# Seven-product couples in the down projection: two or four per FFN group, block products kept in PSUM over a layer

## What is computed

```python
def hybrid_layer(x, ...):
    ...
    x = x + rms_norm(mixed, g_mix_post)
    f = jnp.square(jax.nn.relu(rms_norm(x, g_ffn_pre) @ w_up)) @ w_down
    return x + rms_norm(f, g_ffn_post)

def reference(x, ...):
    for l in range(DEPTH):
        x = hybrid_layer(x, ...)
    return x
```

## Time and profile before

| | |
|---|---|
| median of 3 runs | 1924.66 us (1924.56 to 1925.11) |
| the profiled execution | 1924.85 us, span of its instructions 1923.0 us |
| busy | PE 1904.1 us (99%), VectorE 1376.1 (72%), ScalarE 951.4 (49%), GpSimd 139.6 (7%) |
| mean granted TensorE clock | 0.999 |
| HBM read | 377.55 MB, 197 GB/s over the span |

### The profile page before, as it was taken

How to read it: one execution, slowest core, us unless ns; L and a number is a source line. 1 busy time by engine, 2 the same in 40 slices (tenths; PEclk the granted TensorE clock), 3 DMA queues, 4 the chain that set the end, 5 groups by cost and what they waited for, 6 DMA issues and landing times.

```text
span 1923.0 us, 28285 instructions
## 1 busy us (share of the span) xinstructions
PE 1904.1 (99%) x10070; PEld 1695.4 (88%) x10070; DVE 1376.1 (72%) x1637; ACT 951.4 (49%) x1249; POOL 139.6 (7%) x178
## 2 busy tenths in 40 slices
PE   9999999999999999999999999999999999999998
PEld 7988888888988988898888888889889889989987
DVE  6885767875785686578778757678657757856785
ACT  6455656543453444345454556556434434444452
POOL 3920020000000000000200000200000000000002
PEclk9999999999999999999999999999999999999999
DMA  8665356666666566666476544566766765666664
GB/s 286 207 225 171 125 171 219 198 226 189 190 225 206 177 207 219 182 205 218 159 240 219 182 163 147 186 210 198 228 188 190 227 197 183 205 222 185 200 207 139
DMA packets 168324, 380.78 MB, mean 198 GB/s; under 512 B 11968, under 2 KB 14128, under 8 KB 167728
## 3 DMA queue, kind: packets, MB, share of 16 engines
q1 hardware_dynamic: 167904, 377.58, 61.2%
q10 hardware_dynamic: 336, 2.11, 0.3%
HBM read 377.55 MB, written 2.10 MB: 197 GB/s over the span
## 4 chain that ended last, share of the span: by engine, by line
PE 89%; DVE 6%; issue 2%; ACT 1%; DMA 1%; POOL 0%; DVEq 0%; ACTq 0%; POOLq 0%; SPq 0%
PE acc_pair L530 22%; PE acc_pair L535 11%; PE acc_pair L829 9%; PE acc_pair L831 9%; PE acc_pair L830 9%; PE acc_pair L496 8%; PE acc_pair L498 8%; PE acc_pair L497 8%; DVE w_lo L1319 2%; ACT w_hi L938 1%; DVE act_f L1785 1%; PE o_bank L748 1%; DVE h_both L1373 1%; DVE x L1354 0%; PE t_bank L729 0%
## 5 line engine op out<-in xcount | busy, mean ns | idle before, releaser
L1319 DVE TENSOR_TENSOR w_lo<-raw,w_hi 128x1024 fp32r<-128x1024 f32 x703 | 862.1, 1245 | 352.7 <-ACT w_hi L938 344.1
L938 ACT CAST w_hi<-raw 128x1024 fp32r<-128x1024 f32 x703 | 722.5, 1049 | 504.6 <-PE acc_pair L831 231.1
L530 PE MATMUL acc_pair<-h_both,w_hi 128*128 128x512 f32 x2176 | 561.1, 380 | 5.4 <-DVE act_f L1785 5.3
L530 PEld LDWEIGHTS acc_pair<-h_both,w_hi 128*128 128x128 f32 x2176 | 371.3, 191 | 37.0 <-DVE act_f L1785 6.9
L535 PEld LDWEIGHTS acc_pair<-h_both,w_lo 128*128 128x128 f32 x2176 | 327.6, 191 | 29.0
L535 PE MATMUL acc_pair<-h_both,w_lo 128*128 128x256 f32 x2176 | 330.6, 274 | 0.0
L829 PE MATMUL acc_pair<-w_hi,f_hi 128*128 128x512 f32 x784 | 297.3, 379 | 0.0
L830 PE MATMUL acc_pair<-w_lo,f_hi 128*128 128x512 f32 x784 | 297.3, 379 | 0.0
L831 PE MATMUL acc_pair<-w_hi,f_lo 128*128 128x512 f32 x784 | 297.2, 379 | 0.0
L496 PE MATMUL acc_pair<-w_hi,h_both 128*128 128x512 f32 x444 | 170.5, 384 | 1.4 <-DVE w_lo L1319 1.2
L498 PE MATMUL acc_pair<-w_hi,h_both 128*128 128x512 f32 x444 | 168.3, 379 | 0.0
(11 more groups left out here) (247 smaller groups left out, 1586.1 us busy)
## 6 DMA issues: line engine op xcount, KB each, us to landing
raw<-in_w_up SPq DMA_DIRECT2D x256, 512.0 KB, 4.3
raw<-in_w_down SPq DMA_DIRECT2D x256, 512.0 KB, 4.7
raw<-in_w_in SPq DMA_DIRECT2D x128, 512.0 KB, 4.8
raw<-in_w_out SPq DMA_DIRECT2D x64, 512.0 KB, 5.2
x<-in_x SPq DMA_DIRECT2D x8, 256.0 KB, 7.7
w_pool_s<-in_w_pool SPq DMA_DIRECT2D x2, 1024.0 KB, 7.9
post_row<-in_g_mix_post SPq DMA_DIRECT2D x2, 1024.0 KB, 7.8
post_row<-in_g_ffn_post ACTq DMA_DIRECT2D x2, 1024.0 KB, 8.1
```

Source lines behind the costliest of these rows:

```text
L530: pe.matmul(acc_pair[b][:, m, :], w_hi[:, slot, col:col + P], x_both.rearrange("p s (a n) -> p s n a", a=2), start=(slot, k) == (0, 0), st ...
L938: act.copy(w_hi[:, half * PAIRS + p, :], raw[:, p, :]).then_inc(hi_made, 1)
L1319: dve.tensor_tensor(w_lo[:, slot, :], raw[:, p, :], w_hi[:, slot, :].bitcast(F32), ALU.subtract).then_inc(lo_made, 1)
```

## The change

It puts four couples into the first wide pair, at blocks 0, 4, 8 and 12, with the row blocks reordered so that their f blocks are ready. s tiles get four copies, t tiles stay one set. The four shared products accumulate in their PSUM banks over the four groups of a layer (start in group 0, stop in the last couple of group 3). `p_sums` is gone. In the last group ScalarE copies two of the banks to `q_sum`, and `combine` reads the other two from PSUM; it now stands behind `wide_sums` and two lows. In `seven`, the products that need t tiles come after the four that don't. In up units VectorE does the second bank's reduction after one low in place of two and s_lo; in the last unit the second half's lows move behind all of it, into `seven_lo` of couple 1.

```diff
-SEVEN_AT = (0, RING)
-K_ORDER = ((4, 5, 0, 1, 2, 3, 8, 9, 6, 7, 10, 11, 12, 13, 14, 15), tuple(range(2 * RING)))
+SEVEN_AT = (0, PAIRS, RING, RING + PAIRS)
+SEVEN_UNIT = ((1, 0), (1, 1), (2, 0), (2, 1))
+K_ORDER = ((4, 5, 0, 1, 6, 7, 2, 3, 8, 9, 12, 13, 10, 11, 14, 15), tuple(range(2 * RING)))
...
@@ tensor: seven
-                    first, last = n == 0, n == len(SEVEN_AT) - 1
+                    first = n == 0
+                    p_first = first and isinstance(g, int) and g == 0
+                    p_last = isinstance(g, int) and g == FF_GROUPS - 1 and n == len(SEVEN_AT) - 1
...
-                    pe.wait_ge(t_lo_made, no + 1)
-                    if first and not (isinstance(g, int) and l + g == 0):
-                        pe.wait_ge(p_free, 4 * (l * FF_GROUPS + g))
-                    three(t_bank[1][:, :], sh[:, 0, :], sl[:, 0, :], t_hi[:, 0, :], t_lo[:, 0, :],
-                          first, last)
-                    three(o_bank[:, :], sh[:, 1, :], sl[:, 1, :], t_hi[:, 1, :], t_lo[:, 1, :],
-                          first, last)
...
+                    pe.wait_ge(t_lo_made, no + 1)
+                    three(t_bank[1][:, :], sh[:, 0, :], sl[:, 0, :], t_hi[:, 0, :], t_lo[:, 0, :],
+                          p_first, p_last)
+                    three(o_bank[:, :], sh[:, 1, :], sl[:, 1, :], t_hi[:, 1, :], t_lo[:, 1, :],
+                          p_first, p_last)
...
@@ scalar: turned_unit, group
+                    if (u, 0) in SEVEN_UNIT:
+                        split_hi(hu + 3, 1, (0, 1, 2))
+                        s_rest(g, SEVEN_UNIT.index((u, 0)))
+                        split_hi(hu + 3, 1, (3,))
+                    elif u < CHUNKS - 1:
                         split_hi(hu + 3, 1)
                     turned_hi(g, u, 1)
+                    if u == CHUNKS - 1:
+                        s_rest(g, 3)
+                        seven_hi(g, 1, hu + 3, 1)
...
-                    seven_hi(g, 1, hu + 10)
-                    for n in range(1, PAIR_HALVES if last else 2 * PAIR_HALVES):
+                    seven_hi(g, 2, hu + 10, 0)
+                    seven_hi(g, 3, hu + 11, 1)
+                    for n in range(2, PAIR_HALVES if last else 2 * PAIR_HALVES):
                         split_hi(hu + 8 + n + 2, n % 2)
                     if not last:
                         return
+                    act.wait_ge(t_used, seven_no(l, g, len(SEVEN_AT)))
+                    for k, bank in ((0, t_bank[0]), (1, t_bank[1])):
+                        act.copy(halves(q_sum[:, k, :]), put_back(bank[:, :])).then_inc(p_copied, 1)
...
@@ vector: combine, wide_pair, turned_unit
-                    dve.wait_ge(p_free, 4 * FF_GROUPS * (l + 1))
+                    dve.wait_ge(p_copied, 2 * (l + 1))
+                    for t in range(T):
+                        dve.wait_ge(acc_free[t], 1 + a0 + ACC_F + 8 * FF_GROUPS - 2)
...
-                        seven_lo(g, 1, hu + 2)
-                        split_lo(hu + 3, 1)
-                        split_lo(hu + 4, 0, (0, 1))
-                        p_sums(g, first)
-                        split_lo(hu + 4, 0, (2, 3))
-                        if last:
-                            combine()
+                        seven_lo(g, 2, hu + 2, 0)
+                        seven_lo(g, 3, hu + 3, 1)
+                        split_lo(hu + 4, 0)
...
                     wide_sums(g, j, first)
                     split_lo(hu + PAIR_HALVES + 1, 1, (2, 3))
+                    if last:
+                        combine()
...
-                        split_lo(hu + u * 2 + 3, 1, (1, 2))
-                        if u == 1:
-                            s_rest(g, 0)
+                        if u < CHUNKS - 1:
+                            split_lo(hu + u * 2 + 3, 1, (1,))
                         turned_square(g, u, 1)
-                        split_lo(hu + u * 2 + 3, 1, (3,))
+                        if u < CHUNKS - 1:
+                            split_lo(hu + u * 2 + 3, 1, (2,))
+                        if (u, 0) in SEVEN_UNIT:
+                            s_rest(g, SEVEN_UNIT.index((u, 0)))
+                        if u < CHUNKS - 1:
+                            split_lo(hu + u * 2 + 3, 1, (3,))
                         turned_lo(g, u, 1)
-                        if u == 1:
-                            s_sums(g, 1)
+                        if (u, 1) in SEVEN_UNIT:
+                            s_sums(g, SEVEN_UNIT.index((u, 1)))
+                        if u == CHUNKS - 1:
+                            s_rest(g, 3)
+                            seven_lo(g, 1, hu + u * 2 + 3, 1)
```

More of the change, by code:

```diff
@@ L231, in build @@
     t_lo = at("t_lo", [P, 3, CH], F32R, r_qkv + 24 * CH)
[L232 to L235, removed]
+    r_s = ((r_qkv + 36 * CH, r_qkv + 40 * CH), (r_qkv + 44 * CH, r_xg), (r_xg + 4 * CH, r_post),
+           (r_post + 4 * CH, r_post + 8 * CH))
+    s_hi = [at(f"s_hi{n}", [P, 4, P], F32R, hi) for n, (hi, _) in enumerate(r_s)]
+    s_sum = [at(f"s_sum{n}", [P, 4, P], F32, low) for n, (_, low) in enumerate(r_s)]
+    s_lo = [at(f"s_lo{n}", [P, 4, P], F32R, low) for n, (_, low) in enumerate(r_s)]
     ident = own("ident", [P, P])
@@ L844, in seven @@
                     pe.wait_ge(lo_made, (hu + i // PAIRS) * PAIRS + 2 + RAW)
-                    pe.wait_ge(t_lo_made, no + 1)
-                    if first and not (isinstance(g, int) and l + g == 0):
-                        pe.wait_ge(p_free, 4 * (l * FF_GROUPS + g))
-                    three(t_bank[1][:, :], sh[:, 0, :], sl[:, 0, :], t_hi[:, 0, :], t_lo[:, 0, :],
-                          first, last)
-                    three(o_bank[:, :], sh[:, 1, :], sl[:, 1, :], t_hi[:, 1, :], t_lo[:, 1, :],
-                          first, last)
                     three(ssa_bank[:, :], sh[:, 2, :], sl[:, 2, :], w_hi[:, s0, right],
-                          w_lo[:, s0, right], first, last)
+                          w_lo[:, s0, right], p_first, p_last)
                     three(t_bank[0][:, :], f_hi[:, k0, early], f_lo[:, k0, early], w_hi[:, s0, left],
-                          w_lo[:, s0, left], first, last).then_inc(w_used, 1)
+                          w_lo[:, s0, left], p_first, p_last).then_inc(w_used, 1)
                     if first:
@@ L1229, in s_rest, with seven_hi @@
                     act.copy(s_hi[n][:, :, :], s_sum[n][:, :, :]).then_inc(s_hi_made, 1)
[L1231 to L1235, removed]
+                def seven_hi(g, n, hu, half):
+                    no = seven_no(l, g, n)
+                    act.wait_ge(t_third, no + 1)
+                    split_hi(hu, half, (0, 1))
+                    act.wait_ge(t_step, 3 * no + 3)
                     act.copy(t_hi[:, :, :], t_sum[:, :, :]).then_inc(t_hi_made, 1)
-                    split_hi(hu, 0, (2, 3))
+                    split_hi(hu, half, (2, 3))
                 def turned_unit(g, u, hu):
                     if u == CHUNKS - 1:
-                        seven_hi(g, 0, hu + 2)
+                        seven_hi(g, 0, hu + 2, 0)
                     elif u == 2:
@@ L1853, in s_rest, with seven_lo @@
                                       ).then_inc(s_lo_made, 1)
-                def seven_lo(g, n, hu):
+                def seven_lo(g, n, hu, half):
                     no = seven_no(l, g, n)
@@ L1872, in seven_lo @@
                                       ).then_inc(t_step, 1)
-                    split_lo(hu, 0, (0, 1))
+                    split_lo(hu, half, (0, 1))
                     dve.wait_ge(t_hi_made, no + 1)
@@ L1876, in seven_lo @@
                                       ALU.subtract).then_inc(t_lo_made, 1)
[L1877 to L1888, removed]
+                    split_lo(hu, half, (2, 3))
                 def combine():
                     q1, q5, q6, q7 = (q_sum[:, k, :] for k in range(4))
-                    dve.wait_ge(p_free, 4 * FF_GROUPS * (l + 1))
+                    dve.wait_ge(p_copied, 2 * (l + 1))
+                    for t in range(T):
+                        dve.wait_ge(acc_free[t], 1 + a0 + ACC_F + 8 * FF_GROUPS - 2)
                     def into(t, c, part):
@@ L1898, in into @@
                                                  ALU.mult, ALU.add).then_inc(q_step, 1)
-                    dve.tensor_tensor(q6, q6, q1, ALU.add).then_inc(q_step, 1)
+                    dve.tensor_tensor(halves(q6), put_back(o_bank[:, :]), halves(q1), ALU.add
+                                      ).then_inc(q_step, 1)
                     into(0, 0, q1)
                     dve.wait_ge(q_step, 8 * l + 1)
-                    dve.tensor_tensor(q7, q7, q6, ALU.add).then_inc(q_step, 1)
+                    dve.tensor_tensor(halves(q7), put_back(ssa_bank[:, :]), halves(q6), ALU.add
+                                      ).then_inc(q_step, 1)
                     dve.tensor_tensor(q6, q6, q5, ALU.add).then_inc(q_step, 1)
```

20 lines of the change are left out of this document (8 added, 12 removed).

## The result

| | before | after |
|---|---|---|
| median | 1924.61 us (1924.09 to 1925.11) | 1977.56 us (1976.39 to 1978.26, 4 runs) |
| the profiled execution | 1924.85 us, span 1923.0 | 1976.39 us, span 1974.6 |
| mean granted TensorE clock | 0.999 | 0.985 |

The ratio is 1.0275 [1.0257, 1.0292]: 53 us slower, where 34 were forecast. The time lies in the range, near the 1981 us of rival 1.

A forecast was written before the change was run, and what follows sets the result against it. PE bounds the kernel, by its count of matmuls plus few gaps. Against 1924.85 us: -10.4 (matmuls) -5.3 (up units) +4.8 (couples) +45.0 (standstills) = +34.1, so 1959 us; range 1938 to 1985.

The forecast's parts named there:

- rival 1: PE's clock falls to half pace behind each wide-pair standstill, 2.7 us more each, 22 in all: 1981 us; chance 0.32.
- Matmuls: In the two more couples of each of 8 groups, 48 fewer matmuls take 10.4 us off PE.
- Up units: VectorE reduces unit 1's second bank earlier, closing eight PE gaps of 0.66 us: 5.3 us off.
- Couples: In the first wide pair, PE slips 0.2 us at each of three couples per group: 4.8 us on.
- Standstill: After the first wide pair, PE waits for sums behind six lows: 5.7 us, 5.4 more in last groups; 45.0 on.
- point (e): Expected sign in the trace: a group takes about 170.8 us, against 166.41 before.
- rival 2: Loads land sooner or the chain has slack, so wide-pair standstills shrink to VectorE's own work: 1928 us; chance 0.10.
- The clock: Behind wide-pair standstills, the forecast's own case kept PE at full clock and charged nothing for a fall.
- The last group: In each layer's last group, combine behind the sums stays hidden: 0, at worst 1 us per layer.
- Rival 3: VectorE keeps its lead, lows do not delay the sums; only matmuls and eight gaps count: 1909 us; chance 0.06.

The follow-up runs named there:

- The version of 1913.61 us: Changed kernel with first wide pair's sums after two lows, combine two lows after them, bank copies before most casts, first narrow sum behind one low: 1913.61 us.
- the last experiment: The version of 1913.61 us with block 1's cast and low of each couple moved ahead of VectorE's wait for t_used: 1944.68 us.

## Why the prediction was right in sign and 19 us short

- **Matmuls** (-10.4): right; 48 are gone, and the experiments' sums close with it to within some 2 us.
- **Up units** (5.3): the mechanism was right, the size was not; 7.8. I multiplied the idle time that the rows print. The time lost is start against due start, 0.93 us and not 0.66.
- **Couples** (0.2 us each, 4.8): 0.19 in the mean, 4.5 in all. In the group shown the heads come 10.12 and twice 9.95 us apart (550.08, 560.20, 570.15) against 9.71; the head waits for a low, and `t_lo` for the moved products is hidden, as worked out.
- **Standstill** (5.7 us, in the last groups 5.4): 5.84 by the row, 6.0 from ready to start (5.4 to 6.2 over the eight), at the place and by the chain foretold. VectorE met `t_used` 4.84 us behind the first head and 4.95 behind the second (565.15 against 560.20), where I had 4.8; low 6 ended at W + 45.1 where I had 44.3. From the end of one such gap to that of the next are 173.1 us (422.79, 595.92): the 170.8 of point (e), 1.9 of clock behind the first of them, and 0.4 more. The loads landed as the earlier trace rows had them, in 5.1 us in the median here against 5.0; no run shortened them, so their part in the 6 us rests on the timeline. The Trainium skill's page "DMA: Bandwidth & Descriptors" (Anatomy of one DMA) gives its 2.0 us plus bytes at 436 GB/s for DMAs that GpSimd's path issues, and these loads go by SyncE's hardware queue, which the prediction passed over. With that figure, by my estimate 3.2 us for 512 KB, rival 2 would have come out; the loads of w_down took 4.7 us in the median of the whole run, and the measurement decides.
- **The clock** was the step that failed. The forecast's own case had it at full level behind a standstill, and put 2.7 us each aside as rival 1 (0.32). It happened every time, at 2.25 us: 18.0 of the missing 19. That this one term fills the gap is in part luck: the others were off by -2.5 (up units), -0.3 (couples) and +1.4 us (standstills, with the 0.93 us of a last group), which nearly cancel. Before's only row that bore on it was the program's start, PE idle and then at half pace. It was the nearest row that there was for a PE that had stood idle, and nothing in the trace spoke for the other outcome; it should have carried the likeliest case. The Trainium skill's page "TensorE: Matmul & The Clock Gate" (Part 1) says that an idle PE falls to half rate; here the traces agree for the long gaps, with 0.50 behind each of 5.3 us and more.
- **The last group** (0): right for the change, whose late sums hid `combine`. With the sums early, the same code opened gaps of 9.7 and 10.4 us: "hidden" held only as long as the cover.
- Rival 3 (1909 us) named what a change of this kind can bring when the sums do not hang on the lows. The version of 1913.61 us is that case, with its slips and last-group waits on top.

## What to carry to other kernels

Ask of every in-order queue what stands ahead of the instruction that frees another engine's buffer: two couples more per pair, 1.3 us of matmuls saved, cost 6 us because six lows stood ahead of one sum. Price an idle TensorE at its length and, where the gap is long, the half-paced stretch behind it (1.4 to 2.9 us here), and look for that stretch in the granted clock rather than in the first matmul. When a wait is removed, look again at what it had hidden.

## What the runs showed of the hardware

- The granted clock fell behind all eight gaps of 5.3 to 6.1 us in the change, and cost 1.4 to 2.9 us each. The gaps of 9.70 and 10.39 us (sums behind two lows) cost no more, 1.8 and 2.0 us. All of 3.5 to 4.8 us lost it too. Of shorter gaps, lengths of 2.5 to 3.2 us did both: 2.51 us lost the clock in one place, 3.18 us kept it in another of the same kernel. It fell up to 1.2 us after PE had resumed. In the last experiment it fell behind two gaps of 1.92 us, and kept full level behind fourteen others of 1.6 to 2.4 us. What tells these cases apart stays open.
- VectorE's subtraction for a low (128x1024) takes 1.22 us alone, and 2.2 us each while GpSimd multiplies 128x512 blocks in SBUF (933 to 941 us above). GpSimd's multiplications take 2.0 us each there. That the two engines' access to memory collides is the nearest reading; no run isolated it.
- The idle time that the trace prints before a matmul of 128x512 is 0.16 us less than what the engine lost (5.84 printed, 6.00 lost above), since it counts from the modelled end of the matmul ahead.
